# Indexer weights in the values' chunk, one product for the spatial gate, and a first MLP unit 512 columns wide

## The reference

```python
def swiglu_ffn(h, w_gu, w_down):
    a, b = jnp.split(h @ w_gu, 2, axis=-1)
    return (jax.nn.silu(a) * b) @ w_down

def second_block(x, ...):
    for l in range(DEPTH):
        h = swiglu_ffn(rmsnorm(x, ffn1_pre_g[l]), ffn1_w_gu[l], ffn1_w_down[l])
        x = x + 0.5 * rmsnorm(h, ffn1_post_g[l])
        h = mixing_sublayer(rmsnorm(x, mix_pre_g[l]), w_in[l], ...)
        x = x + rmsnorm(h, mix_post_g[l])
        h = swiglu_ffn(rmsnorm(x, ffn2_pre_g[l]), ffn2_w_gu[l], ffn2_w_down[l])
        x = x + 0.5 * rmsnorm(h, ffn2_post_g[l])
```

```python
z = h @ w_in
uv, pz, qz, kz, vz, qi, ki, wi, cz, gz = jnp.split(z, ...)
# gmlp_mixer: u, v = split(gelu(uv)); v = rmsnorm(v, v_g)
mixed = jnp.einsum('gts,bcsgd->bctgd', wsm, vc) + wb.T[None, None, :, :, None]
# sparse_attention: the score from which the top 64 keys are taken
score = jnp.einsum('bqh,bqhs->bqs', wib, rel)
```

## Time and profile before

| | before |
|---|---|
| timed runs, median (lowest to highest) | 1900.3 us (1900.29 to 1900.43) |
| profiled execution: time / span | 1901.72 us / 1900.0 us |
| TensorE matmul busy | 1892.4 us, 100% |
| VectorE busy | 1410.7 us, 74% |
| ScalarE busy | 899.3 us, 47% |
| GpSimd busy | 233.7 us, 12% |
| DMA | 356.78 MB, mean 188 GB/s |

### The profile page before, as it was taken

The page is one execution under the profiler, slowest core; times in us unless marked ns, Lnnn a source line. Parts: engine busy times, 40 slices in busy tenths (PEclk is TensorE's granted clock), DMA queues, the critical chain, the costliest instruction groups (busy, mean ns, idle before and its releaser), DMA issues.

```text
span 1900.0 us, 26171 instructions
## 1 busy us (share of the span) xinstructions
PE 1892.4 (100%) x10118; PEld 1626.7 (86%) x10118; DVE 1410.7 (74%) x1625; ACT 899.3 (47%) x949; POOL 233.7 (12%) x199
## 2 busy tenths in 40 slices
PE   9999999999999999999999999999999999999998
PEld 7888888888888888888898888888888898888887
DVE  7986866578768666766779787667766779787666
ACT  5554434445544444544645545444444545545443
POOL 0000000000001000000049320000000049320000
PEclk9999999999999999999999999999999999999999
DMA  8545555565456554555444556555555454455553
GB/s 301 189 162 198 189 191 197 177 211 192 170 197 210 198 187 167 211 198 181 164 177 155 177 200 215 185 189 185 203 185 190 162 189 156 171 206 188 189 187 111
DMA packets 51619, 356.78 MB, mean 188 GB/s; under 512 B 6312, under 2 KB 6448, under 8 KB 9680
## 3 DMA queue, kind: packets, MB, share of 16 engines
q1 hardware_dynamic: 47952, 341.93, 51.1%
q0 software_dynamic: 3296, 13.67, 2.1%
q10 hardware_dynamic: 288, 0.04, 0.0%
HBM read 353.50 MB, written 2.11 MB: 187 GB/s over the span
## 4 chain that ended last, share of the span: by engine, by line
PE 99%; DMA 0%; issue 0%; DVEq 0%; ACT 0%; POOLq 0%; POOL 0%; SPq 0%; DVE 0%
PE ps L234 23%; PE ps L309 14%; PE ps L310 14%; PE ps L317 14%; PE ps L239 12%; PE ps L196 4%; PE ps L198 3%; PE ps L197 3%; PE ps L214 1%; PE ps L221 1%; PE ps L215 1%; PE ps L2892 1%; PE ps L2897 1%; PE ps L2893 1%; PE ps L2627 1%; PE ps L1504 1%
## 5 line engine op out<-in xcount | busy, mean ns | idle before, releaser
L172 DVE TENSOR_TENSOR w_lo<-raw,w_hi 128x2048 fp32r<-128x2048 f32 x314 | 720.0, 2298 | 235.9 <-ACT w_hi L165 235.2
L165 ACT ACTIVATE w_hi<-raw 128x2048 fp32r<-128x2048 f32 x314 | 601.0, 1916 | 517.9 <-PE ps L317 246.1
L234 PE MATMUL ps<-a,w_hi 128*128 128x512 f32 x1952 | 464.9, 390 | 0.0
L234 PEld LDWEIGHTS ps<-a,w_hi 128*128 128x128 f32 x1952 | 362.5, 188 | 73.0
L239 PEld LDWEIGHTS ps<-a,w_lo 128*128 128x128 f32 x1952 | 250.3, 191 | 9.5
L239 PE MATMUL ps<-a,w_lo 128*128 128x256 f32 x1952 | 253.2, 283 | 0.0
L309 PE MATMUL ps<-w_hi,a 128*128 128x512 f32 x592 | 233.4, 394 | 0.0
L310 PE MATMUL ps<-w_hi,a 128*128 128x512 f32 x592 | 230.7, 390 | 0.0
L310 PE MATMUL ps<-w_hi,mix 128*128 128x512 f32 x576 | 225.0, 391 | 0.0
L309 PE MATMUL ps<-w_hi,mix 128*128 128x512 f32 x576 | 225.0, 391 | 0.0
L317 PE MATMUL ps<-w_lo,a 128*128 128x512 f32 x592 | 146.4, 389 | 0.0
(11 more groups left out here) (428 smaller groups left out, 2190.5 us busy)
## 6 DMA issues: line engine op xcount, KB each, us to landing
raw<-in_w_b SPq DMA_DIRECT2D x198, 1024.0 KB, 4.9
raw<-in_w_a SPq DMA_DIRECT2D x124, 1024.0 KB, 4.9
rows<-in_post_gains POOLq DMA_DIRECT2D x6, 512.0 KB, 5.1
rows<-in_rows_a POOLq DMA_DIRECT2D x2, 1028.0 KB, 8.0
raw<-in_w_a SPq DMA_DIRECT2D x4, 512.0 KB, 7.1
rows<-in_rows_a POOLq DMA_DIRECT2D x2, 1024.0 KB, 6.7
x<-in_x SPq DMA_DIRECT2D x2, 512.0 KB, 5.8
a_gates<-bias_line POOLq DMA_DIRECT2D x2, 512.0 KB, 6.0
```

Source lines behind the costliest of these rows:

```text
L165: act.activation(k.w_hi[:, s, :], k.raw[:, s, :], ACT.Copy).then_inc(k.hi_ready, 1)
L172: dve.tensor_tensor(k.w_lo[:, s, :], k.raw[:, s, :], k.w_hi[:, s, :].bitcast(F32), ALU.subtract).then_inc(k.lo_ready, 1)
L234: pe.matmul(both, hi[:, kt, n * P:(n + 1) * P], k.a[:, :, kt, :], start=kt == 0, stop=False)
```

## The change

Three edits in the second block, in the words of the diff:

- The first unit of the MLP takes its weights as two chunks that each hold all 512 columns (256 of a, 256 of b) for half of the feature tiles (`mlp_pack`, `first_unit`). One product is 512 columns wide and goes to one bank: tile 0 to bank 0, tile 1 to bank 2. `up0_done` is signalled once, when tile 0 is complete; Silu for tile 1 waits for the second chunk.
- The indexer weights become columns 256 to 259 of the values' chunk. `w_hi` and `w_lo` get room for 32 more columns in each slot; for chunk M0 + 2 ScalarE and VectorE each run a second small instruction that splits the 32 columns of the parameters. The values' product is 260 columns wide, tile 0 in bank 0 and tile 1 in bank 1. The 16 matmuls, ScalarE's copy of 8 rows, the products against the identity, the small splits in the MLP and six semaphores go. VectorE evicts `w_idx` right after the values, and feature 4 waits for that.
- The spatial gate is one product of 128 columns for each of the four groups (two tiles of 64) instead of two of 64.

```diff
-                    ins = dve.tensor_tensor(r, r, k.ps[:, 2 * tt + 1, 0:BW], ALU.mult)
+                    ins = dve.tensor_tensor(r, r, k.ps[:, 2 * tt, BW:2 * BW], ALU.mult)
...
+        def second_high_split(k, act, st, layer, c):
+
+            if c != M0 + 2:
+                split_high(k, act, st, layer, c)
+                return
+            act.wait_ge(k.raw_loaded[c % SLOTS], st.loads(layer, c))
+            act.wait_ge(k.chunk_done, st.count(layer, c))
+            act.activation(values_w[0][:, :, 0:BW], raw_values(c), ACT.Copy)
+            act.activation(values_w[0][:, :, BW:VALUES], wi, ACT.Copy).then_inc(k.hi_ready, 1)
...
+                dve.wait_ge(f_evicted.sem, f_evicted.at(l, 1))
+                for tt in range(TT):
+                    ins = dve.tensor_scalar(w_idx[:, tt, :], k.ps[:, tt, BW:VALUES], rho[:, tt:tt + 1], rho[:, tt:tt + 1],
+                                            ALU.mult, ALU.mult)
+                ins.then_inc(wi_ready.sem, 1)
                 hc = conv_x[:, :, CONV_PAD:]
                 dve.wait_ge(rbc_ready.sem, rbc_ready.at(l, 2))
                 evict(3, hc, hc)
-                dve.wait_ge(wi_summed.sem, wi_summed.at(l, 1))
-                for tt in range(TT):
-                    ins = dve.tensor_scalar(w_idx[:, tt, :], k.ps[:, 6, SEQ + tt * IH:SEQ + (tt + 1) * IH], rho[:, tt:tt + 1],
-                                            rho[:, tt:tt + 1], ALU.mult, ALU.mult)
-                ins.then_inc(wi_ready.sem, 1)
...
-                ca, cb = a_chunk(f, 0), b_chunk(f, 0)
-                pe.wait_ge(k.lo_ready, st.count(l, ca))
-                up_first(ca, 0, 0, range(8)).then_inc(up0_done.sem, 1)
-                pe.wait_ge(k.lo_ready, st.count(l, cb))
-                up_first(cb, 1, 0, range(6))
+                pe.wait_ge(k.lo_ready, st.count(l, F0[f]))
+                first_unit(0, 0, range(4))
+                pe.wait_ge(k.lo_ready, st.count(l, F0[f] + 1))
+                first_unit(1, 0, range(3))
                 x_transpose(l, n, 1, range(1))
-                up_first(cb, 1, 0, range(6, 8)).then_inc(up0_done.sem, 1)
+                first_unit(1, 0, range(3, 4)).then_inc(up0_done.sem, 1)
                 x_transpose(l, n, 1, range(1, 2))
-                up_first(ca, 2, 1, range(8)).then_inc(k.chunk_done, 1)
-                up_first(cb, 3, 1, range(8)).then_inc(k.chunk_done, 1)
+                first_unit(0, 1, range(4)).then_inc(k.chunk_done, 1)
+                first_unit(1, 1, range(4)).then_inc(k.chunk_done, 1)
...
-                t_chunk(k, pe, M0 + 2, range(8), 256, aop, lambda tt, h: k.ps[:, 0, tt * BW:(tt + 1) * BW], True, True)
-                pe.wait_ge(par_loaded.sem, par_loaded.at(l, 32))
-                pe.wait_ge(wi_split.sem, wi_split.at(l, 1))
-                for kt in range(KT):
-                    pe.matmul(k.ps[0:2 * IH, 6, 0:SEQ], wi_both[:, kt, :], k.aH[:, kt, :], start=kt == 0, stop=False)
-                    ins = pe.matmul(k.ps[0:2 * IH, 6, 0:SEQ], wi_both[:, kt, :], k.aL[:, kt, :], start=False, stop=kt == KT - 1)
-                ins.then_inc(wi_done.sem, 1)
+                for tt in range(TT):
+                    for kt in range(KT):
+                        a = [x[:, tt * P:(tt + 1) * P] for x in aop(kt)]
+                        ins = product(pe, k.ps[:, tt, 0:VALUES], a, [w[:, kt, :] for w in values_w], kt == 0, kt == KT - 1)
+                ins.then_inc(k.chunk_done, 1)
...
-                pe.wait_ge(wi_copied.sem, wi_copied.at(l, 1))
-                for tt in range(TT):
-                    out, a = k.ps[:, 6, SEQ + tt * IH:SEQ + (tt + 1) * IH], wi_rows[:, tt * P:(tt + 1) * P]
-                    pe.matmul(out, a, k.ident[0:2 * IH, 0:IH], start=True, stop=False)
-                    ins = pe.matmul(out, a, k.ident[0:2 * IH, IH:2 * IH], start=False, stop=True)
-                ins.then_inc(wi_summed.sem, 1)
                 feature(4)
                 feature(5)
                 pe.wait_ge(vn_ready.sem, vn_ready.at(l, 1))
-                for tt in range(TT):
-                    for g in range(4):
-                        ins = pe.matmul(k.ps[:, 2, tt * BW + g * 64:tt * BW + (g + 1) * 64], ws[:, g, :],
-                                        vn[:, tt, g * 64:(g + 1) * 64], start=True, stop=True)
+                for g in range(4):
+                    ins = pe.matmul(k.ps[:, 2, g * P:(g + 1) * P].rearrange("p (t n) -> p t n", t=TT), ws[:, g, :],
+                                    vn[:, :, g * 64:(g + 1) * 64], start=True, stop=True)
                 ins.then_inc(gm_done.sem, 1)
...
-    chunks = [a[0], b[0]]
+    chunks = t_pack(np.concatenate([gu[:, :256], gu[:, 256 * FF_B:256 * FF_B + 256]], axis=1), 512)
```

More of the change, by code:

```diff
@@ L1729, in second_block @@
                                    ("y0T_done", 1), ("y0H_ready", 1), ("y0_split", 1)))
-        wi_high, wi_split, wi_done, wi_copied, wi_summed, wi_ready, rel_done, rel_ready = (
-            sig(n, 1) for n in ("wi_high", "wi_split", "wi_done", "wi_copied", "wi_summed", "wi_ready", "rel_done", "rel_ready"))
-        wi_rows = score[0:2 * IH, 0:SEQ]
+        wi_ready, rel_done, rel_ready = (sig(n, 1) for n in ("wi_ready", "rel_done", "rel_ready"))
         f_evicted, hc_ready, conv_done, pool_ready, taps_ready, conv_rest = (
@@ L1788, in post_last, with second_low_split @@
             return (M0 - 1, F0[1] - 1, CB - 1)[n]
+        values_slot = (M0 + 2) % SLOTS
+        values_w = [w[:, values_slot, 0:KT * VALUES].rearrange("p (k n) -> p k n", k=KT) for w in (k.w_hi_wide, k.w_lo_wide)]
+        raw_values = lambda c: k.raw[:, c % SLOTS, :].rearrange("p (k n) -> p k n", k=KT)
+        def second_high_split(k, act, st, layer, c):
[6 more added lines that the diff above has]
+            act.activation(values_w[0][:, :, BW:VALUES], wi, ACT.Copy).then_inc(k.hi_ready, 1)
+        def second_low_split(k, dve, st, layer, c):
+            if c != M0 + 2:
+                split_low(k, dve, st, layer, c)
+                return
+            dve.wait_ge(k.hi_ready, st.count(layer, c))
+            dve.tensor_tensor(values_w[1][:, :, BW:VALUES], wi, values_w[0][:, :, BW:VALUES].bitcast(F32), ALU.subtract)
+            dve.tensor_tensor(values_w[1][:, :, 0:BW], raw_values(c), values_w[0][:, :, 0:BW].bitcast(F32), ALU.subtract)\
+               .then_inc(k.lo_ready, 1)
         @block.gpsimd
@@ L2045, in _ @@
             for l in range(DEPTH):
-                high = Splitter(split_high, k, act, st, l, AHEAD_HIGH)
+                high = Splitter(second_high_split, k, act, st, l, AHEAD_HIGH)
                 act.wait_ge(par_loaded.sem, par_loaded.at(l, 32))
@@ L2275, in mlp @@
                 split_low(k, dve, st, l, F0[f] + 4)
-                if f == 0:
-                    dve.wait_ge(wi_high.sem, wi_high.at(l, 1))
-                    dve.tensor_tensor(wi_lo, wi, wi_hi.bitcast(F32), ALU.subtract).then_inc(wi_split.sem, 1)
                 def scale(j, trips=0, q=0):
@@ L2322, in _ @@
             for l in range(DEPTH):
-                low = Splitter(split_low, k, dve, st, l, 2)
+                low = Splitter(second_low_split, k, dve, st, l, 2)
                 ch = Chain(dve_chain.sem, DVE_B)
@@ L2954, in tensors @@
     k.raw = sb("raw", [P, SLOTS, CH])
-    k.w_hi, k.w_lo = sb("w_hi", [P, SLOTS, CH], F32R), sb("w_lo", [P, SLOTS, CH], F32R)
+    k.w_hi_wide, k.w_lo_wide = (sb(n, [P, SLOTS, CH + KT * IH], F32R) for n in ("w_hi", "w_lo"))
+    k.w_hi, k.w_lo = k.w_hi_wide[:, :, 0:CH], k.w_lo_wide[:, :, 0:CH]
     k.x = sb("x", [P, TT, DM])
```

41 lines of the change are left out of this document (18 added, 23 removed).

## The result

| | before | after |
|---|---|---|
| timed, median of nine (lowest to highest) | 1900.34 us (1900.14 to 1900.53) | 1905.53 us (1905.27 to 1907.26) |
| span of the profiled execution | 1900.0 us | 1903.8 us |
| TensorE matmul busy | 1892.4 us | 1895.8 us |
| matmuls | 10118 | 9862 |

The account below looks back on a forecast made before the run. TensorE, busy for 1892.4 of 1900.0 us, was taken to bound the kernel. Gains of 1.86 (MLPs) and 6.88 (mixing) less 0.16 (VectorE wait) made 8.6 us: 1900.3 - 8.6 = 1891.7 us, range 1889.9 to 1894.7.

Parts of the forecast that it names:

- no penalty for an odd width or pitch: Values' 260-column products: four added columns cost 1.7 ns each product, 0.08 us, judged from rows of 65 against 64 columns.
- Rival C: Values' 260-column products might each need a second pass, 120 ns more on 96 products: 1903.2 us, slower; chance 0.03.
- Parts 2 and 3: Indexer weights and spatial gate in each layer's mixing: TensorE gains 3.44 us a layer, 6.88 in two.
- Values and indexer weights: Mixing: removing 16 products with 8-column stationary operand saves 1.83 us; added columns in the values' products cost 0.08.
- Around the sums: Mixing: removing the products that add the indexer weights' halves saves 0.98 us a layer.
- Spatial gate: Mixing: four products of 128 columns replace eight of 64, gaining 0.71 us a layer (bounds 0.5 and 0.85).
- Part 1: First unit of four MLPs: pairs of 256-column products merged at 11.9 ns saved each, 1.86 us (bounds 1.4 and 2.3).
- The wait at the second chunk: First MLP unit: TensorE waits for the second chunk's low half, charged 0.10 us in three MLPs (bounds 0 and 0.25).
- Rival B: First MLP units: wide products save nothing, that edit comes to minus 0.3 us, time 1893.9 us; chance 0.10.
- gate 16 of layer 0: TensorE, 3.44 us early, waits for VectorE's low split, which moves only 3.28 us: 0.16 us given back.
- the same gate in layer 1: VectorE's split for gate 16 ends 0.8 us before TensorE wants it: nothing is lost.
- rival A: VectorE, slowed beside GpSimd's convolution work, takes back 1 to 3 us before the gates: 1892.7 to 1894.7 us; chance 0.20.

Follow-up runs that it names:

- e9: Changed kernel with slots back 8192 bytes apart and 64 columns behind the last slot of w_hi and w_lo, same instructions; against after and before: 1892.59 us, ratio 0.9962.
- e1: Kernel before with only w_hi and w_lo slots lengthened by 32 unused columns, instructions unchanged: 1914.75 us, ratio 1.0075.
- e16: Kernel before with only the MLPs' first unit made 512 columns wide, layout of before: 1898.71 us against 1900.15, ratio 0.9994.
- e4: Kernel before with the 512-wide first MLP unit and the merged spatial gate, without the indexer-weights edit or wider slots: 1898.30 us against 1900.06, ratio 0.9991.
- e15: As e9, but GpSimd does 4 of its 16 convolution taps in each layer and leaves 12 out: 1890.40 us, 2.2 us under e9.
- e12: As e5, with w_hi and w_lo 64 bytes further: 1903.84 us, one run.
- e13: As e9, but w_lo (not w_hi) 64 bytes further: 1898.71 us, ratio 0.9993.
- e3: Changed kernel with 32 columns behind the last slot only and tensors reordered; w_lo landed 32 bytes off the intended place: 1907.43 us, ratio 1.0038.
- e6: As e5, with w_hi and w_lo 128 bytes further: 1929.30 us, one run.
- e11: Kernel before with 128 unused bytes between w_lo and x, so the activations move against the weights: 1929.90 us.
- e14: As e13, but with w_lo 192 bytes further than in e9: 1904.80 us, one run.
- e10: Kernel before with 128 unused bytes ahead of all tensors, so every start moves and all distances stay: 1900.05 us.
- e2: Kernel before with 768 unused bytes between w_lo and x, so the activations move and the weights stay: 1900.38 us, ratio 1.0002.
- e5: Kernel before with x, a and mix placed ahead of w_hi and w_lo, all at multiples of 8192 bytes: 1901.83 us, one run.
- e7: As e5, with w_hi and w_lo 256 bytes further: 1901.16 us, one run.
- e8: Kernel before with w_hi and w_lo placed ahead of raw, the activations staying where they were: 1900.27 us, one run.

## Why the prediction was wrong, step by step

**The step that failed** is one without a price. The edit "`w_hi` and `w_lo` get room for 32 more columns in each slot" stands in the change; the prediction weighed a pitch of 260 only for the 96 products of the values, "no penalty for an odd width or pitch", and gave the moved slots, `w_lo` and all behind it no term at all. In after 6479 products of 512 columns have one operand in these slots, and 0 to 6 ns on each by its slot, 2 ns on average, is 12.9 us here (after less e9) and 14.7 us on the instructions of before (e1): half as much again as the forecast gain of 8.6. Rows 8 compare 65 with 64 columns of short products, and could not have shown it; nothing in the trace of before could, since every slot stands a multiple of 256 bytes from the activations there. The prediction gave 0.02 to the outcome that came, slower. But the question "which addresses does this move, and who reads them" would have named a cost with open bounds, and the range should have held it.

**Rival C** had the right sign and place in the diff (a wider weight tile), not the mechanism: the 260-column products cost 120 ns (L196 to L198 mean 119 to 120 in after, 117 to 121 in e9), just under the 121 to 122 of the prediction. It was priced for 96 products where the cost sat in over sixty times as many.

**Parts 2 and 3**, with the distances kept. Timeline of PE in e9, mixing of layer 0:

```profile
945.78 0.28 PE L196 MATMUL ps<-w_hi,a 128*128 128x260 f32 x1
...
951.50 0.63 PE L234 MATMUL ps<-a,w_hi 128*128 128x512 f32 x2
...
957.06 0.61 PE L2780 MATMUL ps<-consts 128*128 128x128 f32 x4
957.43 0.70 PE L234 MATMUL ps<-a,w_hi 128*128 128x512 f32 x2
...
968.66 1.06 PE L2786 MATMUL ps<-GU,rows 128*128 128x128 f32 x8
969.48 0.48 PE L234 MATMUL ps<-a,w_hi 128*128 128x512 f32 x1
```

The two rows of before that it needs beside the earlier trace rows:

```profile
947.98 0.28 PE L196 MATMUL ps<-w_hi,a 128*128 128x256 f32 x1
...
961.11 0.61 PE L2766 MATMUL ps<-consts 128*128 128x128 f32 x4
```

- Values and indexer weights: (955.56 - 947.98) - (951.50 - 945.78) = 7.58 - 5.72 = 1.86 us; forecast 1.83 - 0.08 = 1.75.
- Around the sums: (962.63 - 961.11) - (957.43 - 957.06) = 1.52 - 0.37 = 1.15; forecast 0.98. The other 0.17 lies in the four records ahead: 961.65 - 961.11 = 0.54 us up to the sums in before, 0.37 up to the next feature in e9. Why is not shown.
- Spatial gate: 1.70 - (969.48 - 968.66) = 0.88; forecast 0.71, and the upper bound 0.85 was too low. The price was taken from the earlier trace rows, where what follows the eighth record starts 0.205 us behind it; behind the gate of e9 it starts after 0.03 us.

Together 3.89 us a layer where 3.44 were forecast, 0.9 us more in two.

**Part 1** was 0.4 us too high: 1.47 by the trace of e16 (1.44 timed), forecast 1.86. The wait at the second chunk came out as charged; timeline of e16, second MLP:

```profile
1137.98 0.49 PE L196 MATMUL ps<-w_hi,a 128*128 128x512 f32 x1
1138.31 0.40 PE L197 MATMUL ps<-w_lo,a 128*128 128x512 f32 x1
1138.55 0.40 PE L198 MATMUL ps<-w_hi,a 128*128 128x512 f32 x1
```

1137.98 to 1138.31 is 0.33 us where 0.227 is the rule: 0.10. But behind such a break products of 512 columns are not at 227 ns at once: here they start 0.22 to 0.24 apart for some ten products, before they settle. The earlier trace rows were taken from a stretch that had nearly settled (its first three starts are 228 to 233 ns apart, the rest 226.7), while a first unit has four breaks (the second chunk, two groups of transposes, the start). The four MLPs have 180 merged pairs on the path (24 and 21 in each); with 0.3 us of waits added back they saved 1.77 us, some 10 ns a pair against the 11.9 of the earlier trace rows. Rival B is out. By the isolated gap of the Trainium skill ("TensorE: Matmul & The Clock Gate", Back-to-back issue gap), columns over 2.4 plus 2.5 ns, a merged pair would save 2.5 ns, by this estimate 0.45 us for the 180; e16 with its 10 ns a pair doesn't agree.

**What becomes late next.** The wait that the prediction charged, gate 16 of layer 0 with 0.16 us, did not come: in after and e9 its low products start when the high ones are done. The one that it put at nothing, the same gate in layer 1 ("0.8 us in hand, nothing is lost"), did: 0.69 us in e9, which is one of its own signs of being wrong. And at a place that it did not look at, the transposes of the convolution in layer 0, TensorE waited 1.15 us by the starts. Timelines of GpSimd and PE of before:

```profile
1057.42 3.21 POOL L1877 TENSOR_TENSOR conv_y<-conv_y,sum 128x512 f32<-128x512 f32 x1 [10.66 <-DVE conv_y L2409]
...
1060.85 0.60 PE L2864 MATMUL ps<-consts,conv_y 128*128 128x128 f32 x4
```

GpSimd ends at 1060.63, TensorE asks at 1060.85: 0.22 us in hand, behind a chain of VectorE's taps. How that chain moved is in VectorE's timelines of layer 0, before and then e9:

```profile
1044.09 4.54 DVE L2409 SCALAR_TENSOR_TENSOR conv_y<-conv_x,rows,conv_y 128x256 f32<-128x256 f32 x6
...
1050.75 1.66 DVE L2409 SCALAR_TENSOR_TENSOR conv_y<-conv_x,rows,conv_y 128x256 f32<-128x256 f32 x4
```

```profile
1037.28 4.98 DVE L2424 SCALAR_TENSOR_TENSOR conv_y<-conv_x,rows,conv_y 128x256 f32<-128x256 f32 x6
...
1045.48 1.66 DVE L2424 SCALAR_TENSOR_TENSOR conv_y<-conv_x,rows,conv_y 128x256 f32<-128x256 f32 x4
```

The values start 947.98 - 945.78 = 2.20 us sooner in e9. The low split of gate 16 starts 1035.58 - 1028.78 = 6.80 us sooner, so VectorE had moved by 4.6 us there and not by 3.28: the shift helped. In e4, without part 2, the split starts only 1.64 us sooner than in before, and TensorE waits 0.61 us for it. Behind it the six taps and the split of the lines above take 6.81 - 5.27 = 1.54 us longer in e9 than in before: 0.44 in the taps, 1.10 in the split that starts 0.13 us behind a GpSimd addition. That is rival A with its mechanism. In size the waits are 1.15 + 0.69 = 1.8 us by the starts, and e15 gains 2.2 without GpSimd's taps (forecast of A: 1 to 3 us), though A was only a rival beside a forecast of 0.16.

**The sum again.** By the trace of e9: mixing 3.86 and 3.94, MLPs 1.54, waits and small shifts behind them -0.9 and -0.8: 7.6 us, and the medians say 1900.20 - 1892.59 = 7.61. The forecast of 8.6 for these parts was 1.0 too high: part 1 by 0.3, the waits by some 1.6, less 0.9 from parts 2 and 3. That e9 comes within 1 us of the forecast is partly luck, since the last error made up for more than half of the waits. The layout then took 12.9. That is less than the 14.7 of e1, probably because the slower TensorE of after is no longer early at the convolution and at gate 16: its list of waits has neither, and 14.7 less the 1.8 us of waits is 12.9. This fits by size and was not tested.

**Still open:** why the distance counts, how the cost depends on it between 0 and 256 bytes (32, 64, 128 and 192 were run, each in some pairs of tensors only), and why L239 differs between e12 and e13.

## What to carry to other kernels

A tensor that grows moves every tensor behind it, and with slots inside it the slots themselves. Ask of each edit which start addresses it changes and which of the most frequent instructions read from there, and keep the distances between the operands of matmuls where they were; padding to the next multiple of 256 bytes cost nothing here and was worth 12.9 us. When untouched code gets slower in a trace, test the layout alone first: one run (e1) did it.

Where an engine is at 100%, look at every hand-over to it within a few microseconds behind the edit, not only at the one that already waits: the next wait was at a GpSimd instruction with 0.22 us in hand.

## What the runs showed of the hardware

- A float32 product of 512 columns starts every 226.7 ns in a settled run if the two operands start a multiple of 256 bytes apart in their partitions, and every 229 to 234 ns (mean) if they are 32 (e3), 64 (e12, e13), 128 (e6, e11) or 192 bytes (e14) off. With 128 bytes it doesn't matter which of the two is moved (e6, e11), and moving both costs nothing (e10: 1900.05 us), nor does a shift by a multiple of 256 bytes (e2, e5, e7, e8).
- With 256 moving columns (L239) the sign turns: 119.5 ns at distance 0, 118.7 to 118.8 at 128, and at 64 bytes 113.9 in one layout (e12) and 118.0 in another (e13).
- Products of 512 columns also need some steps to settle with the best distance. Behind products of 256 columns the first five take 234, 236, 228, 232 and 231 ns (means of 122 runs of before), then 226.7; behind a wait or transposes it takes some ten, of 224 to 240 ns.
- The Trainium skill ("SBUF — State Buffer", SBUF: two separate sides) has TensorE wait for no other engine at SBUF. No run here tests that. In line with it, in after the low products of 35 units of the second block's MLPs have a spacing of 229.4 to 229.6 ns, whatever the other engines do, and the cost changes with the distance of TensorE's own operands.
- GpSimd's work makes VectorE's longer: the same 1625 instructions keep VectorE busy for 1412.6 us beside all of GpSimd's taps (e9) and for 1389.1 us beside a quarter of them (e15).
